# Output-projection weight splits ahead of the query copies, key and value copies in another order, and narrower waits of the first two attention heads

## What is computed

```
def mla_mixer(h, positions, w_in, q_norm, kv_norm, w_uq, w_ukv, w_o):
    ...
    proj = h @ w_in
    cq = rms_norm(proj[..., :MLA_Q_RANK], q_norm)
    ckv = rms_norm(proj[..., MLA_Q_RANK:MLA_Q_RANK + MLA_KV_RANK], kv_norm)
    k_rope_in = proj[..., MLA_Q_RANK + MLA_KV_RANK:]
    q = (cq @ w_uq).reshape(bsz, seq, MLA_HEADS, MLA_QK)
    kv = (ckv @ w_ukv).reshape(bsz, seq, MLA_HEADS, MLA_NOPE + MLA_V)
    k_nope, v = kv[..., :MLA_NOPE], kv[..., MLA_NOPE:]
    ...
        s = jnp.einsum('bqhd,bkhd->bhqk', q_blk, k, preferred_element_type=jnp.float32) * sm_scale
        s = jnp.where(key_idx[None, :] <= q_idx[:, None], s, -jnp.inf)
        p = jax.nn.softmax(s, axis=-1).astype(v.dtype)
        return jnp.einsum('bhqk,bkhd->bqhd', p, v)
    ...
    return o @ w_o
```

## Time and profile before

| | us |
|---|---|
| median of 3 runs | 1126.92 |
| lowest and highest of them | 1125.61, 1130.12 |
| profiled execution | 1127.26 |
| its span, first to last instruction | 1125.2 |
| TensorE busy | 1026.1 (91%) |
| TensorE weight loads, beside the products | 850.1 (76%) |
| VectorE busy | 824.1 (73%) |
| ScalarE busy | 621.6 (55%) |

### The profile page before, as it was taken

One profiled execution on the slowest core, in us unless ns is written; L12 is line 12 of the kernel. 1 busy time (PEld: TensorE's weight loads), 2 busy tenths in 40 slices (PEclk: granted clock), 3 DMA queues, 4 the chain that ended last, 5 costly groups with the idle time before them and its releaser, 6 DMA issues.

```text
span 1125.2 us, 18126 instructions
## 1 busy us (share of the span) xinstructions
PE 1026.1 (91%) x6880; PEld 850.1 (76%) x6881; DVE 824.1 (73%) x1116; ACT 621.6 (55%) x764; POOL 29.6 (3%) x73
## 2 busy tenths in 40 slices
PE   0777799999999999879989999999999999999993
PEld 0554488898989888656778888888888888888882
DVE  7899885354353448578377898888989898898874
ACT  4421265343343445456356777768686776867662
POOL 3000000000000000000100000000000000000000
PEclk9976789999999999989989999999999999999997
DMA  9847894296878776240437999999999999999951
GB/s 265 327 161 232 256 332 148 90 359 227 293 253 302 257 264 244 87 149 1 132 111 260 362 335 349 318 352 321 349 335 338 351 313 348 326 349 337 329 193 58
DMA packets 199110, 293.00 MB, mean 260 GB/s; under 512 B 18293, under 2 KB 164970, under 8 KB 198778
## 3 DMA queue, kind: packets, MB, share of 16 engines
q1 hardware_dynamic: 189114, 283.32, 73.2%
q10 hardware_dynamic: 8160, 5.85, 1.8%
q0 software_dynamic: 1760, 2.78, 1.0%
HBM read 287.39 MB, written 2.11 MB: 257 GB/s over the span
## 4 chain that ended last, share of the span: by engine, by line
issue 52%; PE 30%; DVE 10%; DMA 3%; ACT 2%; SPq 2%; POOL 0%; DVEq 0%; ACTq 0%; POOLq 0%
PE ps L588 7%; PE ps L589 7%; PE ps L590 7%; PE ps L632 2%; PE ps L660 1%; DMA raw<-in_w_ada 1%; DMA mod_rows<-ada_wide 1%; SPq L408 1%; DVE w_lo L1532 1%; DMA raw<-in_ffn_w_in 1%; PE ps L954 1%; ACT w_hi L1169 1%; PE ps L945 1%; PE ps L743 1%; PE ps L937 1%
## 5 line engine op out<-in xcount | busy, mean ns | idle before, releaser
L2045 DVE TENSOR_TENSOR w_lo<-raw,w_hi 128x2048 fp32r<-128x2048 f32 x162 | 366.0, 2287 | 65.8 <-ACT w_hi L1449 65.8
L1449 ACT ACTIVATE w_hi<-raw 128x2048 fp32r<-128x2048 f32 x162 | 304.0, 1911 | 0.0
L1532 DVE TENSOR_TENSOR w_lo<-raw,w_hi 128x2048 fp32r<-128x2048 f32 (+3 forms) x59 | 131.6, 2249 | 112.1 <-ACT w_hi L1169 110.7
L588 PE MATMUL ps<-w_hi,xe_hi 128*128 128x512 f32 x448 | 180.4, 403 | 1.6 <-DVE xe_lo L2022 1.6
L590 PE MATMUL ps<-w_hi,xe_lo 128*128 128x512 f32 x448 | 175.7, 392 | 0.0
L589 PE MATMUL ps<-w_lo,xe_hi 128*128 128x512 f32 x448 | 174.6, 390 | 0.0
L1169 ACT ACTIVATE w_hi<-raw 128x2048 fp32r<-128x2048 f32 (+3 forms) x59 | 109.3, 1879 | 96.3 <-DMA raw<-in_ffn_w_in 77.2
L588 PE MATMUL ps<-act_hi,w_hi 128*128 128x256 f32 x352 | 102.4, 291 | 1.9 <-DVE act_lo L1700 1.5
L589 PE MATMUL ps<-act_lo,w_hi 128*128 128x256 f32 x352 | 100.1, 284 | 0.0
L590 PE MATMUL ps<-act_hi,w_lo 128*128 128x256 f32 x352 | 100.1, 284 | 0.0
L590 PEld LDWEIGHTS ps<-w_hi,xe_lo 128*128 128x128 f32 x448 | 84.1, 188 | 18.7
(11 more groups left out here) (394 smaller groups left out, 1633.5 us busy)
## 6 DMA issues: line engine op xcount, KB each, us to landing
raw<-in_moe_w_in SPq DMA_DIRECT2D x224, 512.0 KB, 5.4
raw<-in_moe_w_out SPq DMA_DIRECT2D x56, 1024.0 KB, 7.3
raw<-in_w_ada SPq DMA_DIRECT2D x48, 1024.0 KB, 9.3
raw<-in_ffn_w_in SPq DMA_DIRECT2D x44, 512.0 KB, 7.9
raw<-in_ffn_w_out SPq DMA_DIRECT2D x11, 1024.0 KB, 11.5
raw<-in_ssm_w_glu SPq DMA_DIRECT2D x16, 512.0 KB, 7.7
raw<-in_mla_w_o SPq DMA_DIRECT2D x4, 1024.0 KB, 6.2
raw<-in_mla_w_uq SPq DMA_DIRECT2D x3, 768.0 KB, 7.1
```

What stands on the lines that cost most here:

```text
L588: mm(dst, st[0], mv[0], start=first, stop=False)
L1449: af(HI[:, (V_MOE + m) % RING, :], RAW[:, (RAW_OF_W[V_MOE] + m) % RING, :], cp).then_inc(hi_done, 1)
L1532: tt_(LO[:, slot, 0:w], RAW[:, RAW_OF_W[v] % RING, 0:w], HI[:, slot, 0:w].bitcast(F32), ALU.subtract)\
L2045: tt_(LO[:, slot, :], RAW[:, (RAW_OF_W[V_MOE] + m) % RING, :], HI[:, slot, :].bitcast(F32), ALU.subtract)\
```

## The change

On ScalarE and VectorE, units 8 to 10 are split ahead of the query copies (`split_to(V_MLA + 11)` in the place of `+ 8`) and unit 11 behind them (`+ 12` in the place of `+ 9`); no split is left between the key/value copies and the head loop. Behind that split ScalarE has a new exponential of one column, whose result nobody reads. ScalarE's eight key and value copies come in two groups: key of b = 0, key and value of b = 2, key and value of b = 3; then, after the copy of head 0's transposed queries and keys, key of b = 1 and the values of b = 0 and 1. The copies count on one semaphore for each token tile (`kv0_ok` for ScalarE's, `kv1_ok` for VectorE's) in the place of one for keys and one for values. VectorE's copies keep their order.

On TensorE, the first tile of the key/value projection waits for two query copies only before b = 2. The wait for all sixteen copies goes to head 2; head 0 waits for three of ScalarE's and one of VectorE's copies, head 1 for five and one, and their scores for two and four of VectorE's.

```
--- before.py
+++ after.py
@@ -286,8 +286,8 @@
         f_mm, f_silu, f_prod, f_hi, f_lo = sems("f_mm f_silu f_prod f_hi f_lo")
         x_out, p_sb, p_rt, p_nrm, p_ps, p_f32, p_hi, p_lo = sems(
             "x_out p_sb p_rt p_nrm p_ps p_f32 p_hi p_lo")
-        cs_arg, cs_ok, q_sb, q_rope, k_rope, kf_ok, vv_ok = sems(
-            "cs_arg cs_ok q_sb q_rope k_rope kf_ok vv_ok")
+        cs_arg, cs_ok, q_sb, q_rope, k_rope, kv0_ok, kv1_ok = sems(
+            "cs_arg cs_ok q_sb q_rope k_rope kv0_ok kv1_ok")
         qk_ps, qk_sb, s_mm, s_max, e_ok, pn_ok, pt_ps, pt_sb, o_mm, o_hi, o_lo = sems(
             "qk_ps qk_sb s_mm s_max e_ok pn_ok pt_ps pt_sb o_mm o_hi o_lo")
         rc_in, tri_ok, lg_ps, td_ok, te_ok, msk_ok, pos_ps, hot_ok, ovf_ok = sems(
@@ -908,19 +908,25 @@
                 wait_unit(v)
                 w = unit(v, "p n -> p n")
                 for tt in range(TT):
-                    if k == 0:
-                        pe.wait_ge(q_sb, (2, 6)[tt])
+                    if k == 0 and tt:
+                        pe.wait_ge(q_sb, 6)
                     for b in range(4):
+                        if k == 0 and tt == 0 and b == 2:
+                            pe.wait_ge(q_sb, 2)
                         last = mm3(PS[:, (6 + 4 * tt + b) % 8, :], [x[:, 3 + k, tt * P:(tt + 1) * P] for x in (CQH, CQL)],
                                    [x[:, b * 512:(b + 1) * 512] for x in w], k == 0, k == 1)
                 last.then_inc(unit_used, 1)
 
             pe.wait_ge(k_rope, 2 * TT)
             pe.wait_ge(q_rope, TT)
-            pe.wait_ge(kf_ok, 8)
-            pe.wait_ge(vv_ok, 8)
 
             def head_transpose(h):
+                if h < 2:
+                    pe.wait_ge(kv0_ok, 3 + 2 * h)
+                    pe.wait_ge(kv1_ok, 1)
+                if h == 2:
+                    pe.wait_ge(kv0_ok, 8)
+                    pe.wait_ge(kv1_ok, 8)
                 if h >= 2:
                     pe.wait_ge(qk_sb, h - 1)
                 for i, src in enumerate((Q, KF)):
@@ -931,6 +937,8 @@
             def head_scores(h):
                 b = h % 2
                 pe.wait_ge(qk_sb, h + 1)
+                if h < 2:
+                    pe.wait_ge(kv1_ok, 2 + 2 * h)
                 if h >= 2:
                     pe.wait_ge(s_max, h - 1)
                 mm(PS[:, 2 + b, 0:P], QKT[:, b, 0, 0:P], QKT[:, b, 1, 0:P], start=True, stop=True)
@@ -1362,7 +1370,7 @@
             for i in range(5):
                 act.wait_ge(p_f32, i + 1)
                 af(CQH[:, i, :], C32[:, i, :], cp).then_inc(p_hi, 1)
-            split_to(V_MLA + 8)
+            split_to(V_MLA + 11)
             act.wait_ge(unit_used, V_MLA + 6)
             act.wait_ge(x_out, 16)
             for tt in range(TT):
@@ -1371,14 +1379,24 @@
                 for b in range(3):
                     af(Q[:, tt, :, :].rearrange("p h d -> p (h d)")[:, b * 512:(b + 1) * 512], PS[:, 3 * tt + b, :], cp)\
                         .then_inc(q_sb, 1)
-            split_to(V_MLA + 9)
+            split_to(V_MLA + 12)
+            af(ST[:, 23:24], EPSC[:, :], ACT.Exp)
             act.wait_ge(unit_used, V_MLA + 8)
-            for b in range(4):
+
+            def kv_copy(b, value):
+
                 kv = PS[:, (6 + b) % 8, :].rearrange("p (h d) -> p h d", h=4)
-                af(KF[:, 0, 4 * b:4 * b + 4, 0:NOPE], kv[:, :, 0:NOPE], cp).then_inc(kf_ok, 1)
-                af(VV[:, 0, 4 * b:4 * b + 4, :], kv[:, :, NOPE:], cp).then_inc(vv_ok, 1)
-            split_to(V_MLA + 12)
+                if value:
+                    af(VV[:, 0, 4 * b:4 * b + 4, :], kv[:, :, NOPE:], cp).then_inc(kv0_ok, 1)
+                else:
+                    af(KF[:, 0, 4 * b:4 * b + 4, 0:NOPE], kv[:, :, 0:NOPE], cp).then_inc(kv0_ok, 1)
+
+            for b, value in ((0, 0), (2, 0), (2, 1), (3, 0), (3, 1)):
+                kv_copy(b, value)
             for i in range(H + 5):
+                if i == 1:
+                    for b, value in ((1, 0), (0, 1), (1, 1)):
+                        kv_copy(b, value)
                 if i < H:
                     act.wait_ge(qk_ps, i + 1)
                     if i >= 2:
@@ -1913,20 +1931,19 @@
                 link_(rotate(kr, kr, tt, 1))
                 v_.tensor_copy(KF[:, tt, :, NOPE:], kr.broadcast_to([P, H, ROPE])).then_inc(k_rope, 2)
             dve.wait_ge(k_rope, 4)
-            split_to(V_MLA + 8)
+            split_to(V_MLA + 11)
             for tt in range(TT):
                 if tt:
                     dve.wait_ge(q_rope, tt)
                 dve.wait_ge(q_sb, 3 * (tt + 1))
                 qr = Q[:, tt, :, NOPE:]
                 rotate(qr, qr, tt, H).then_inc(q_rope, 1)
-            split_to(V_MLA + 9)
+            split_to(V_MLA + 12)
             dve.wait_ge(unit_used, V_MLA + 8)
             for b in range(4):
                 kv = PS[:, 2 + b, :].rearrange("p (h d) -> p h d", h=4)
-                v_.tensor_copy(KF[:, 1, 4 * b:4 * b + 4, 0:NOPE], kv[:, :, 0:NOPE]).then_inc(kf_ok, 1)
-                v_.tensor_copy(VV[:, 1, 4 * b:4 * b + 4, :], kv[:, :, NOPE:]).then_inc(vv_ok, 1)
-            split_to(V_MLA + 12)
+                v_.tensor_copy(KF[:, 1, 4 * b:4 * b + 4, 0:NOPE], kv[:, :, 0:NOPE]).then_inc(kv1_ok, 1)
+                v_.tensor_copy(VV[:, 1, 4 * b:4 * b + 4, :], kv[:, :, NOPE:]).then_inc(kv1_ok, 1)
             dve.wait_ge(mask_ok, 1)
             dve.wait_ge(q_rope, 2)
             for i in range(H + 5):
```

## The result

| | before | changed |
|---|---|---|
| median of four runs, us | 1128.51 | 1117.85 |
| lowest to highest, us | 1125.61 to 1130.12 | 1114.66 to 1118.4 |
| profiled execution, us | 1127.26 | 1114.66 |
| its span, us | 1125.2 | 1112.5 |

The ratio is 0.9907, with a 95% interval of 0.9879 to 0.9934: 10.5 us faster, between 7.4 and 13.7. The fourth run of the kernel before moved its median up by 1.6 us, so the agreement of 1117.85 with the forecast of 1117.8 is closer than that of the gains, 10.7 against 9.1; so close a meeting of the times is in part luck.

A forecast was written before the change was run, and what follows sets the result against it. TensorE was busiest, but the bound was the 14.47 us chain of splits, copies and table load before the first probability transpose. Saving 0.9 plus 8.2, 9.1 us in all, takes 1126.9 to 1117.8, range 1114.0 to 1122.0.

The forecast's parts named there:

- The gap: Between key/value projection results and first probability transpose: 14.47 us shrinks to 6.3, saving 8.2 us.
- The hiding: Three splits moved under the query projection fit in idle time of ScalarE and VectorE, costing 0 to 0.5 us.
- The early projection: Key/value projection starts before the second query copy; 0.92 of the 1.27 us wait is kept.
- The table load: One-column exponential pulls the 1.28 us load behind the fourth split, into ScalarE's idle time; the switch costs 1.3 us.
- The sum: First probability transpose to output projection comes 9.1 us sooner: 0.9 from the projection, 8.2 from the gap.
- The expert loads: Issued earlier, during the query projection; the extra traffic costs 0, at most 0.5 us.
- the fourth split: Placed behind the query copies and their rotation, where the first stood, before both engines wait.
- the later stages' order: Behind the output projection's start each engine's order is unchanged, so the gain passes through.
- (a): Rival: clock stays low in the first heads, costing 2 to 4 us, so 1120 to 1122; chance 0.18.
- (b): Rival: third split holds query copies or a table reloads in the loop; 1.3 to 3 us lost; chance 0.09.
- (e): Rival: nothing moves, because something behind the heads ends at a fixed time; 1126.9 us; chance 0.03.
- (d): Rival: slower, sparse transposes keep the clock at 1.2 GHz into the head loop; up to 1141 us; chance 0.02.

The follow-up runs named there:

- wide_waits: The changed kernel with the waits of heads 0 and 1 and the copy order as before; 59.16 us from first query copy to output projection, ratio 0.9929.
- splits_only: The kernel before with only the splits moved; 62.20 us from first query copy to output projection, ratio 0.9932.
- splits_back: The changed kernel with three splits put back between copies and heads; 61.90 us from first query copy to output projection, ratio 0.9947.
- no_table: The changed kernel without the one-column exponential behind the fourth split; 56.85 us from first query copy to output projection.
- warm_q: The changed kernel with 24 products of the identity ahead of the query projection; median 1118.55 us.
- warm_q11_router: The changed kernel with 11 products of the identity ahead of the query projection and extra ones between the router's narrow products; median 1118.66 us.
- after_third: The changed kernel run again unchanged as a yardstick; median 1116.79 us, ratio 0.9909.
- wide_warm: wide_waits with 16 products of the identity ahead of head 0's transposes; 58.68 us from first query copy to output projection.
- wide_warm8: wide_warm with 8 products of the identity in the place of 16; 57.13 us from first query copy to output projection.

## Why the prediction was right

**The gap** was the main term, and its steps hold in order. I worked out 6.26 us from the first key copy to the first probability transpose; measured 6.30. Head 0 came 1.19 us behind the copies instead of 1.06, its scores at 2.49 instead of 2.36. (The timeline names VectorE's key copy as what ended head 0's wait. By the counts only VectorE's first one matters, and it was done at 483.31; ScalarE's third copy ended last, at 483.82.) **The hiding** held, though the query projection ran at the full clock here and so left VectorE less room: 0.64 us before the rotation instead of 1.3. ScalarE had 2.10 us idle before the query copies, as worked out. **The early projection** gave 0.84 instead of 0.92 us; the wait before the second tile, 0.29 us, is the one foretold (0.5), and the two products behind it are 0.1 us further apart than in a stream. **The table load** is hidden, and is worth 1.40 us where I had 1.3. **The sum** of 9.1 is 9.02 in the stretch. The expert loads, the fourth split and the later stages' order cost nothing that can be seen: from the first probability transpose to the output projection it is 37.56 us against 37.57.

**The rivals.** (a), the low clock in the first heads, didn't come up in the changed kernel. Its price of 2 to 4 us fits: 2.03 us in wide_waits, all on the path to the first probability transpose, for which I had 1.2, and 1.75 in the head loop of splits_only, for which I had 1.7. What decided was the idle time ahead of head 0. The three kernels with 2.9 us of it unfilled (before, splits_only, wide_waits) all lost the clock, those with 1.2 us kept it unless a second idle time followed, as the 5.15 us of splits_back. (At other places shorter ones lost it too in some profiles, see the last section.) I had counted the narrow waits only as waits. Had I asked which idle time they remove, I would have found that more than half of their worth is the clock, and that without them the change would have fallen 3.7 us short of its 9. (b) and (e) didn't occur. (d) didn't either: the trickle of the first heads was 4.37 us of work in 5.

**What is open.** The three comparisons give 10.3 to 11.7 us, the stretch gives 9.0. The remainder of 1.3 to 2.7 us lies within the intervals of two of three. But it stands in all runs compared with the kernel before, and for two of them it is beyond the interval: by the ratios splits_only is 7.7 us faster (5.5 to 9.8) where its stretch gives 2.3, splits_back 6.0 (4.1 to 7.8) where it gives 2.6; wide_waits 8.0 (5.3 to 10.7) against 5.3, no_table 9.4 (7.0 to 11.7) against 7.6. So outside the stretch the kernel before loses 1 to 5 us against every variant, and what it is doesn't follow from the edits. The clock may be part of it: its mean over the executions is 0.959 in the kernel before and 0.962 in splits_only, by an estimate from these up to 3 us. In the profile of before, the part behind the start of the output projection took 587.60 us, in the three profiles of the changed kernel 585.1 to 586.0; its clock in the router and at the end differs from execution to execution. Nearly all other variants lie there too, splits_only with 585.64; warm_q (587.50) and warm_q11_router (587.23) don't. About 1.05 us of the 1.85 build up evenly over the expert stage, where the products follow each other every 229.5 ns on average in the kernel before and every 229.0 in the other profiles, splits_only with the same code there among them. With one profile of the kernel before, I can't say whether this belongs to the kernel or to the execution.

## What to carry to other kernels

Work that stands between a producer and the first consumer is worth moving under an earlier matrix stage, but the moved work's own time is not the gain: in the stretch measured here splits alone gave 2.3 us, all other parts without them 2.6, together 9.0. Work the new chain out to the first event in regular rhythm, instruction by instruction. Give every idle time of TensorE that is near 3 us two prices, that of the waiting and that of the clock behind it; splitting one wait into several narrow ones may pay more through the second. To judge a change of under 1%, measure a stretch that begins behind the clock's accidents, and then see whether the whole time agrees; here it gives 1 to 5 us more than the stretch.

## What the runs showed of the hardware

- An idle time of 2.9 to 3.2 us ahead of a matrix stage let the granted clock fall to 0.50 in 3 of 3 profiles at the heads and in 9 of 11 at the query projection, for about 3.4 or 6.8 us there and for 7 to 10 at the heads. The Trainium skill (TensorE: Matmul & The Clock Gate, HAM oscillation — how this bites in real kernels) tells of the same, there for waits of about 3 to 5 us for loads: waits between bursts of products throttle the clock again.
- Shorter idle times are no safe ground. The changed kernel kept 1.00 through the first heads in all its profiles (4.37 us of work in 5 in the first). But behind an idle time of 1.4 us at the start of the input projection 3 of 14 profiles fell to 0.50 for 3.4 us (after_third, wide_warm, wide_warm8), and 1 of 14 (warm_q) at the start of the output projection behind idle times of at most 0.93 us. The Trainium skill (TensorE: Matmul & The Clock Gate, A second HAM failure mode: psum-queue depth-cycling) says that frequent short idle times between groups make the clock go to and fro; these four falls agree with it, the first heads don't.
- A filler of eight products of the identity (2.02 us in 2.9 us of idle time) was enough to keep it in the one profile that has it; sixteen took 3.81 us, not 1.8, since a float32 product of 128 columns is two instructions.
- A product behind an idle time takes 0.47 to 0.50 us with 0.3 us to the next, where in a stream it is 0.39 at a pitch of 0.23.
